# RMS norm weights multiplied before the transposes, evictions by PSUM bank, and tile-by-tile norm between two encoder layers

## Chip, cores and metric

One NeuronCore of a Trainium2 chip (trn2). The metric is device time in microseconds (us) of one execution; lower is better.

## The reference

A two-layer encoder over 256 tokens of width 1024, all in float32. Layer 0 mixes tokens by windowed attention, layer 1 by a gated MLP ("sg", spatial gating); each is followed by a PEER expert mixer. Five RMS norms stand in it, called z = 0 to 4 here: before attention, before the first PEER, before the gated MLP, before the second PEER, and at the end.

```python
def rms_norm(x, g):
    y = xf * lax.rsqrt(jnp.mean(xf * xf, axis=-1, keepdims=True) + NORM_EPS)
    return (y * g).astype(x.dtype)

h = x
for i in range(2):
    hn = rms_norm(h, mix_norm_g[i])
    h = h + (windowed_gqa_attention(hn, ...) if i == 0 else chunked_spatial_gating(hn, ...))
    h = h + peer(rms_norm(h, ffn_norm_g[i]), peer_w_query[i], peer_sub_keys[i], peer_down[i], peer_up[i])
return rms_norm(h, final_norm_g)
```

## The kernel before

The 256 tokens are two tiles (`t` = 0, 1) of 128. Weights stream through the core as "units" of 128 x 1024 numbers, 636 in all. For each unit SyncE (SP) starts a 512 KB transfer into `raw`, ScalarE (ACT) rounds it to `w_hi` (L471), VectorE (DVE) subtracts to get the rest `w_lo` (L725, or L733 in halves), and TensorE (PE) multiplies three times (L1306 to L1308: hi by hi, hi by lo, lo by hi). `w_hi` and `w_lo` have four buffers each. The semaphores `hi_done`, `lo_done` and `used` count units cast, split and multiplied; a unit's buffers come free with `used`. Each engine runs its own instruction list, in the order written, and waits on these counts.

The activations are wanted transposed, also as a hi and a lo part. A norm goes so, with `h` as [tokens, 1024]:

- ACT squares tile 0 and half of tile 1 (L479, L486), DVE the other half (L748), DVE adds epsilon (L744, L751), GpSimd (POOL) takes the power -1/2 (L375, function `root`).
- DVE scales each tile in two halves of 512 columns into `scaled` (L768, `to_scaled`).
- PE transposes 16 blocks of 128 x 128 into PSUM (L1356, `norm_turn`), tile 0 first. At z = 1 and 3 sixteen throw-away transposes (L1346, `fill`) go ahead; at z = 2 they stand between the two tiles.
- For each of eight blocks of 128 columns of `h` (index k), over both tiles, ACT multiplies the PSUM block by the norm's weight (a value per partition, from the small tensor `gains`) and rounds it to `x_hi` (L494), and DVE multiplies again and subtracts into `x_lo` (L779). TURN_ORDER goes through k as 0, 2, 1, 3, ... and ACT waits for DVE's last but one, so that the two read different PSUM banks. PE's first unit takes k in the same order and waits for each `x_lo`.

Around the norms, these queues matter. At the start SP loads `x`, a small table, then weight units. In the attention stage POOL issues the loads of the PEER keys and 28 transfers of 512 KB that clear the `gates` table in DRAM (L388), each paced by `used`; after norm z = 1 four more, and then the store `h_kept` (L432) of 1 MB. DVE overwrites that memory with PEER scores (L1100) and first waits for the store. In the last PEER units of layer 0 (`up` stage), PE takes the last four units for tile 0 first and then for tile 1. The residual (L791) of a tile follows, then norm z = 2, then the "v stage" of the gated MLP: 24 units in six columns of four (`v_columns`), both tiles in each unit.

## Time and profile before

| | |
|---|---|
| runs | 1921.91, 1924.6, 1925.65 us; median 1924.6 |
| profiled execution | 1923.52 us, its span in the trace 1921.7 us |
| busy | PE 98%, DVE 73%, ACT 52%, POOL 36% of the span |
| chain that ended last | PE 80%, ACT 6%, DVE 5%, issue 4%, POOL 4% |
| HBM traffic | 218 GB/s over the span |

The profile is one execution. Its page gives busy time by engine and the costliest groups of instructions, and names for each wait what released it. "L779" is line 779 of the kernel. The granted clock (PEclk) is a share of TensorE's 2.4 GHz: 1.00 or 0.50.

### The profile page before, as it was taken

What the parts mean: (1) busy time and instruction counts of PE and PEld (TensorE: products, weight loads), DVE (VectorE), ACT (ScalarE), POOL (GpSimd) and SP (SyncE); (2) the same over time, 40 slices, a digit from 0 to 9 for tenths busy, and PEclk for the clock granted to TensorE, in tenths of its full rate; (3) what the DMA queues carried; (4) which work ended last, traced back from release to release, by engine and by line L of the source; (5) the groups of instructions that cost most, each with busy time, mean ns of one, the idle gap of its engine ahead of it and who ended that gap; (6) DMA issues with size and microseconds to landing.
All of it is one profiled execution on the core that took longest, in us unless ns stands there. A gap on an engine that the chain in (4) does not pass through costs nothing.

```text
span 1921.7 us, 39006 instructions
## 1 busy us (share of the span) xinstructions
PE 1874.9 (98%) x12114; PEld 1703.6 (89%) x12114; DVE 1397.5 (73%) x3258; ACT 1007.6 (52%) x1638; POOL 696.9 (36%) x627
## 2 busy tenths in 40 slices
PE   7989999999999999999999999999999999999998
PEld 6879999999988888888889989999999988888887
DVE  5858788897467766667567778788897457667666
ACT  4644656656455455454444444666656454454453
POOL 1416687788730000000102106688788740000000
PEclk9999999999999999999999999999999999999999
DMA  6964565565568778996848844566565568778775
GB/s 233 340 249 154 177 185 177 174 179 185 185 217 250 240 240 276 292 304 213 279 159 303 308 155 153 177 185 179 172 186 179 183 206 257 240 239 242 240 241 190
DMA packets 159589, 419.99 MB, mean 219 GB/s; under 512 B 32427, under 2 KB 66251, under 8 KB 159020
## 3 DMA queue, kind: packets, MB, share of 16 engines
q1 hardware_dynamic: 130556, 369.23, 60.7%
q0 software_dynamic: 28976, 50.17, 7.7%
q8 instruction: 16, 0.26, 0.1%
q14 instruction: 41, 0.34, 0.1%
HBM read 382.30 MB, written 37.00 MB: 218 GB/s over the span
## 4 chain that ended last, share of the span: by engine, by line
PE 80%; ACT 6%; DVE 5%; issue 4%; POOL 4%; DMA 1%; SPq 0%; DVEq 0%; POOLq 0%; ACTq 0%
PE psum L1306 26%; PE psum L1308 25%; PE psum L1307 25%; POOL gates L405 4%; ACT L620 2%; ACT w_hi L471 2%; DVE w_lo L733 2%; ACT L662 1%; PE psum L1505 1%; PE psum L1476 1%; ACT big L620 1%; PE psum L1394 0%; DVE big L791 0%; PE psum L1405 0%; PE psum L1431 0%
## 5 line engine op out<-in xcount | busy, mean ns | idle before, releaser
L471 ACT CAST w_hi<-raw 128x1024 fp32r<-128x1024 f32 x636 | 662.9, 1048 | 341.7 <-PE psum L1308 328.8
L1306 PE MATMUL psum<-x_hi,w_hi 128*128 128x256 f32 x2576 | 738.6, 287 | 16.2 <-DVE w_lo L733 13.0
L1307 PE MATMUL psum<-x_lo,w_hi 128*128 128x256 f32 x2576 | 731.2, 284 | 0.0
L1308 PE MATMUL psum<-x_hi,w_lo 128*128 128x256 f32 x2576 | 731.2, 284 | 0.0
L405 POOL DMA_INDIRECT gates<-whole,address x512 | 622.4, 1216 | 246.7 <-issue 148.1
L1306 PEld LDWEIGHTS psum<-x_hi,w_hi 128*128 128x128 f32 x2576 | 496.6, 193 | 27.2 <-issue 12.9
L733 DVE TENSOR_TENSOR w_lo<-raw,w_hi 128x512 fp32r<-128x512 f32 x576 | 369.9, 683 | 178.9 <-ACT w_hi L471 178.5
L1307 PEld LDWEIGHTS psum<-x_lo,w_hi 128*128 128x128 f32 x2576 | 496.8, 193 | 0.9
L1308 PEld LDWEIGHTS psum<-x_hi,w_lo 128*128 128x128 f32 x2576 | 496.4, 193 | 0.0
L1306 PE MATMUL psum<-w_hi,l_hi 128*128 128x512 f32 x1152 | 452.2, 393 | 3.2 <-DVE l_lo L1233 2.2
L1308 PE MATMUL psum<-w_hi,l_lo 128*128 128x512 f32 x1152 | 448.8, 390 | 0.0
L1307 PE MATMUL psum<-w_lo,l_hi 128*128 128x512 f32 x1152 | 448.7, 389 | 0.0
L725 DVE TENSOR_TENSOR w_lo<-raw,w_hi 128x1024 fp32r<-128x1024 f32 x348 | 420.7, 1218 | 18.4 <-ACT w_hi L471 18.4
L652 ACT ACTIVATE big<-psum 128x256 f32<-128x256 f32 x256 | 98.5, 385 | 309.3 <-PE psum L1308 307.0
L1306 PEld LDWEIGHTS psum<-w_hi,l_hi 128*128 128x128 f32 x1152 | 216.7, 188 | 48.7 <-issue 3.9
L1308 PEld LDWEIGHTS psum<-w_hi,l_lo 128*128 128x128 f32 x1152 | 216.5, 188 | 45.4
L1307 PEld LDWEIGHTS psum<-w_lo,l_hi 128*128 128x128 f32 x1152 | 216.7, 188 | 43.8
L1222 DVE TENSOR_TENSOR l_lo<-big,l_hi 128x256 fp32r<-128x256 f32 x248 | 105.5, 425 | 193.5 <-ACT l_hi L670 193.4
L457 POOL DMA_DIRECT2D big<-h_kept x4 | 2.2, 554 | 354.9 <-PE psum L1308 354.9
L1217 DVE TENSOR_TENSOR big<-big,g_t 128x256 f32 (+1 forms) x248 | 103.5, 417 | 5.0 <-DMA g_t<-gates 4.9
L388 POOL DMA_DIRECT2D gates<-zeros x64 | 48.4, 759 | 160.4 <-PE psum L1308 153.7
L670 ACT CAST l_hi<-big 128x256 fp32r (+1 forms) x248 | 98.3, 397 | 0.0
(144 smaller groups left out, 1122.8 us busy)
## 6 DMA issues: line engine op xcount, KB each, us to landing
raw<-in_down SPq DMA_DIRECT2D x256, 512.0 KB
raw<-in_up SPq DMA_DIRECT2D x256, 512.0 KB
raw<-in_sg_units SPq DMA_DIRECT2D x72, 512.0 KB
gates<-zeros POOLq DMA_DIRECT2D x64, 512.0 KB, 7.0
g_t<-gates SPq DMA_DIRECT2D x248, 128.0 KB, 4.5
raw<-in_query SPq DMA_DIRECT2D x32, 512.0 KB
raw<-in_attn_units SPq DMA_DIRECT2D x20, 512.0 KB
gates<-whole,address POOLq DMA_INDIRECT x512
```

The costliest lines, as they stand in the source:

```text
L405: pool.indirect_dma_start(flat, bass.IndirectOffsetOnAxis(address[:, TOPK * m + k:TOPK * m + k + 1], 0), whole[:, t, head, k:k + 1], None, ...
L471: act.copy(w_hi[n % SPLIT][:, :], raw[n % RAW][:, :]).then_inc(hi_done, 1)
L620: act.activation(vals[:, item % 2, :], top1[:, item % 2, :], ACT.Exp, bias=least[:, item % 2:item % 2 + 1], accum_out=sums[:, item % 2:ite ...
L652: act.activation(acts[:, bass.ds(i * group + n, 1), :], p1[n % P1_BANKS].rearrange("p (o t) -> p o t", o=1), ACT.Gelu_apprx_tanh).then_inc ...
L670: act.copy(l_hi[n % GROUP][:, :].rearrange("p (o t) -> p o t", o=1), acts[:, bass.ds(i * GROUP + n, 1), :]).then_inc(l_hi_done, 1)
L725: dve.tensor_tensor(w_lo[n % SPLIT][:, :], raw[n % RAW][:, :], w_hi[n % SPLIT][:, :].bitcast(F32), ALU.subtract).then_inc(lo_done, 1)
L733: ins = dve.tensor_tensor(w_lo[n % SPLIT][:, c], raw[n % RAW][:, c], w_hi[n % SPLIT][:, c].bitcast(F32), ALU.subtract)
L1217: dve.tensor_tensor(a, a, g_t[n % G_TILES][:, :].rearrange("p (o t) -> p o t", o=1), ALU.mult).then_inc(gated_up, 1)
L1222: dve.tensor_tensor(l_lo[n % GROUP][:, :].rearrange("p (o t) -> p o t", o=1), acts[:, bass.ds(i * GROUP + n, 1), :], l_hi[n % GROUP][:, :] ...
L1306: pe.matmul(out_ap, hi_s, hi_m, start=start, stop=False)
L1307: pe.matmul(out_ap, hi_s, lo_m, start=False, stop=False)
L1308: return pe.matmul(out_ap, lo_s, hi_m, start=False, stop=stop)
```

## The change

1. The norm weight is no longer applied after the transposes. A row of 1024 weights, copied to all 128 partitions (`gain_row`, 512 KB), is multiplied in `to_scaled`, by an operation with two tensor inputs. That row is loaded anew for each norm: by SP at the start (z = 0), else by POOL. The small `gains` load is gone.
2. `x_hi` is then a plain copy and `x_lo` a plain subtraction, four of each with 512 columns where there were eight with 256. TURN_ORDER and ACT's wait for DVE are gone; PE waits once per two k.
3. Between the layers, tile 0 is scaled, transposed and split alone. Its transposes stand in PE's list before the last unit's tile 1. The v stage's first column runs tile 0 through units 0 to 3, with tile 1's transposes ahead of unit 3, and then tile 1 through the four units. The sixteen throw-away transposes at z = 2 are gone. The split of v unit 0 is done on POOL, between its two roots, and DVE's next split waits for it.
4. The v stage's first pass is written out on ACT and DVE rather than run as a loop's first turn.

```diff
             for t in range(TT):
                 sp.dma_start(h[:, t, :], x[t * P:(t + 1) * P, :]).then_inc(x_landed, 16)
+            sp.dma_start(gain_row, gains[0].partition_broadcast(P)).then_inc(first_gain_landed, 16)
...
-            pool.dma_start(gains[:, :, :], mix_g).then_inc(const_landed, 16)
...
+            def load_gains(z):
+
+                pool.wait_ge(scaled_done, 4 * z)
+                pool.dma_start(gain_row, gains[z].partition_broadcast(P)).then_inc(gain_landed, 16)
...
             load_keys(0)
+            load_gains(1)
...
-                    roots()
+                    load_gains(3)
...
+                pool.wait_ge(used, up + GAIN_COLUMN + D // T)
+                pool.dma_start(gain_row, (final_g if layer else gains[2]).partition_broadcast(P)).then_inc(gain_landed, 16)
...
+                if layer == 0:
+                    root(slice(0, 1))
+                    n0 = unit0[1]["mix"]
+                    pool.wait_ge(hi_done, n0 + 1)
+                    pool.tensor_tensor(w_lo[n0 % SPLIT][:, :], raw[n0 % RAW][:, :], w_hi[n0 % SPLIT][:, :].bitcast(F32),
+                                       ALU.subtract).then_inc(lo_done, 1)
+                    root(slice(1, 2))
...
-                    dve.tensor_scalar(scaled[:, t, cols], h[:, t, cols], stat[:, 1, t:t + 1], None, ALU.mult
-                                      ).then_inc(scaled_done, 1)
+                    dve.scalar_tensor_tensor(out=scaled[:, t, cols], in0=h[:, t, cols], scalar=stat[:, 1, t:t + 1],
+                                             in1=gain_row[:, cols], op0=ALU.mult, op1=ALU.mult).then_inc(scaled_done, 1)
...
-                    act.wait_ge(turned, 4 * z + k // 2 + 1)
-                    if at > 1:
-                        act.wait_ge(xl_done, KD * z + at - 1)
-                    act.activation(x_hi[:, k, :], turn_at(z, k), ACT.Copy, scale=gains[:, z, k:k + 1]).then_inc(xh_done, 1)
+                    act.wait_ge(turned, TURN_GROUPS * z + at + 1)
+                    source, (k, tok) = turned_part(z, at)
+                    act.copy(x_hi[:, k, tok], source).then_inc(xh_done, 1)
...
-                    dve.scalar_tensor_tensor(out=x_lo[:, k, :], in0=turn_at(z, k), scalar=gains[:, z, k:k + 1],
-                                             in1=x_hi[:, k, :].bitcast(F32), op0=ALU.mult, op1=ALU.subtract
-                                             ).then_inc(xl_done, 1)
+                    dve.tensor_tensor(x_lo[:, k, tok], source, x_hi[:, k, tok].bitcast(F32), ALU.subtract).then_inc(xl_done, 1)
...
+                    def first_column():
+                        for n in range(4):
+                            pe.wait_ge(lo_done, u["mix"] + n + 1)
+                            v_part(n, 0, n % 2 == 0)
+                            if n == 2:
+                                pe.wait_ge(xl_done, TURN_GROUPS * 2 + 2)
+                                turn_tile(2, 1)
+                        for n in range(4):
+                            v_part(n, 1, n % 2 == 0).then_inc(used, 1)
...
                 for c in range(NK - GROUP, NK):
+                    if layer < DEPTH - 1 and c == NK - 1:
+                        turn_tile(2, 0)
                     tile_rows(u["up"] + c, c % GROUP, 1, False, c == NK - 1).then_inc(used, 1)
```

What this does to the order of instructions is seen at three places between the layers. First PE's list, from the last products of the `up` stage (`l_hi`, `l_lo`) to the first of the v stage (`x_hi`), before:

```order
L1307 MATMUL psum<-w_lo,l_hi 128x512
L1308 MATMUL psum<-w_hi,l_lo 128x512
L1356 MATMUL psum<-ident,big 128x128 x8
L1346 MATMUL psum<-ident,x_lo 128x128 x16
L1356 MATMUL psum<-ident,big 128x128 x8
L1306 MATMUL psum<-w_hi,x_hi 128x512
```

And in the changed kernel, where L1350 to L1352 are the three products and L1398 the transposes:

```order
L1352 MATMUL psum<-w_hi,l_lo 128x512
L1398 MATMUL psum<-ident,big 128x128 x8
L1350 MATMUL psum<-w_hi,l_hi 128x512
L1351 MATMUL psum<-w_lo,l_hi 128x512
L1352 MATMUL psum<-w_hi,l_lo 128x512
L1350 MATMUL psum<-w_hi,l_hi 128x512
L1351 MATMUL psum<-w_lo,l_hi 128x512
L1352 MATMUL psum<-w_hi,l_lo 128x512
L1350 MATMUL psum<-w_hi,x_hi 128x512
```

Tile 0's transposes moved ahead of six products of the last unit, the fill is gone, and tile 1's transposes now stand 18 products later, ahead of v unit 3.

Second DVE's list, from the step that starts tile 0's root, before (L748 and L751 are the sum of squares of tile 1):

```order
L744 TENSOR_SCALAR stat<-stat 128x1 [waits sq_done,h_done]
L725 TENSOR_TENSOR w_lo0<-raw0,w_hi0 128x1024 [waits hi_done]
L768 TENSOR_SCALAR big<-big,stat 128x512 [waits rstd_done]
L768 TENSOR_SCALAR big<-big,stat 128x512
L791 TENSOR_TENSOR big<-psum,big 128x512 [waits y_done]
L791 TENSOR_TENSOR big<-psum,big 128x512 [waits used]
L748 ISA big,stat<-big 128x512 [waits h_done]
L748 ISA stat 128x1
L751 SCALAR_TENSOR_TENSOR stat<-stat 128x1 [waits sq_done,d]
L725 TENSOR_TENSOR w_lo1<-raw1,w_hi1 128x1024 [waits hi_done]
L768 TENSOR_SCALAR big<-big,stat 128x512 [waits rstd_done]
```

In the changed kernel, from the same step after tile 0's two scalings (L803 scales, L815 makes `x_lo`, L756 splits, L825 is the residual, L779 and L782 the squares):

```order
L815 TENSOR_TENSOR x_lo<-psum,x_hi 128x4x128 [waits xh_done] x2
L756 TENSOR_TENSOR w_lo1<-raw1,w_hi1 128x1024 [waits hi_done,lo_done]
L825 TENSOR_TENSOR big<-psum,big 128x512 [waits y_done]
L825 TENSOR_TENSOR big<-psum,big 128x512 [waits used]
L779 ISA big,stat<-big 128x512 [waits h_done]
L779 ISA stat 128x1
L782 SCALAR_TENSOR_TENSOR stat<-stat 128x1 [waits sq_done,d]
L756 TENSOR_TENSOR w_lo2<-raw2,w_hi2 128x1024 [waits hi_done]
L803 SCALAR_TENSOR_TENSOR big<-big,stat 128x512 [waits rstd_done]
L803 SCALAR_TENSOR_TENSOR big<-big,stat 128x512
L756 TENSOR_TENSOR w_lo3<-raw3,w_hi3 128x1024 [waits hi_done]
L815 TENSOR_TENSOR x_lo<-psum,x_hi 128x4x128 [waits xh_done] x2
```

The split of v unit 0 left DVE; two halves of `x_lo` and the split of unit 1 now stand ahead of tile 1's residual, and the splits of units 2 and 3 around tile 1's scaling.

Third POOL's list around its two roots, before:

```order
L457 DMA big<-h_kept 128x1024 [waits used] x2
L375 TENSOR_TENSOR stat<-stat,neg_half 128x1 [waits ms_done,rstd_done] x2
L388 DMA gates<-zeros 128x4x256 [waits used] x8
L375 TENSOR_TENSOR stat<-stat,neg_half 128x2 [waits ms_done,rstd_done]
L388 DMA gates<-zeros 128x4x256 [waits used] x24
```

And in the changed kernel (L384 the roots, L479 the split, L396 and L471 loads of weight rows):

```order
L471 DMA big<-in_gains 128x1024 [waits used]
L474 DMA big<-h_kept 128x1024 [waits used] x2
L384 TENSOR_TENSOR stat<-stat,neg_half 128x1 [waits ms_done,rstd_done]
L479 TENSOR_TENSOR w_lo<-raw,w_hi 128x1024 [waits hi_done]
L384 TENSOR_TENSOR stat<-stat,neg_half 128x1 [waits ms_done,rstd_done]
L396 DMA big<-in_gains 128x1024 [waits scaled_done]
L402 DMA gates<-zeros 128x4x256 [waits used] x8
```

A weight row is loaded ahead of `h_kept`, another after the roots, and the split stands between the roots.

## Rows read from the trace of the kernel before

**Rows 1.** The page, part 1: busy time (share of span) and instructions.

```profile
PE 1874.9 (98%) x12114; PEld 1703.6 (89%) x12114; DVE 1397.5 (73%) x3258; ACT 1007.6 (52%) x1638; POOL 696.9 (36%) x627
```

**Rows 2.** Groups by line: busy us, mean ns of one | idle before them, releaser.

```profile
L494 ACT ACTIVATE x_hi<-psum,gains 128x256 fp32r<-128x256 f32 x32 | 13.8, 472 | 12.4 <-PE psum L1356 9.0 <-DVE x_lo L779 3.3 <-issue 0.2
L768 DVE TENSOR_SCALAR big<-big,stat 128x512 f32<-128x512 f32 x16 | 7.2, 502 | 1.2 <-POOL stat L375 1.2
...
L773 DVE SCALAR_TENSOR_TENSOR big<-big,stat 128x512 f32<-128x512 f32 x4 | 2.8, 748 | 1.5 <-POOL stat L375 1.5
L791 DVE TENSOR_TENSOR big<-psum,big 128x512 f32<-128x512 f32 x16 | 10.5, 686 | 3.5 <-PE psum L1308 3.4
L539 ACT COPY big<-psum 128x512 f32<-128x512 f32 x16 | 9.2, 577 | 10.9 <-PE psum L1405 10.8
```

**Rows 3.** Timeline of the start: start us, us, instruction [idle before, releaser].

```profile
10.41 1.05 ACT L471 CAST w_hi<-raw 128x1024 fp32r<-128x1024 f32 x1 [1.74 <-DMA raw<-in_attn_units]
...
12.83 0.88 DVE L779 SCALAR_TENSOR_TENSOR x_lo<-psum,gains,x_hi 128x256 fp32r<-128x256 f32 x2
...
13.46 0.55 PE L1306 MATMUL psum<-x_hi,w_hi 128*128 128x256 f32 x1 [1.10 <-DVE x_lo L779]
...
13.92 0.88 DVE L779 SCALAR_TENSOR_TENSOR x_lo<-psum,gains,x_hi 128x256 fp32r<-128x256 f32 x2 [0.21 <-ACT x_hi L494]
...
17.87 0.38 PE L1308 MATMUL psum<-x_hi,w_lo 128*128 128x256 f32 x1
18.08 0.28 PE L1306 MATMUL psum<-x_hi,w_hi 128*128 128x256 f32 x1
...
32.70 0.69 DVE L818 SCALAR_TENSOR_TENSOR big<-psum,big 128x512 f32<-128x512 f32 x1 [1.79 <-PE psum L1394]
```

**Rows 4.** Windows: stretch, length, POOL busy, PEclk, DMA share, GB/s.

```profile
112.00:116.00 4.00, 0.95 (x2) 1.00 0.99 371
116.00:120.00 4.00, 1.29 (x2) 1.00 0.33 97
```

**Rows 5.** Timeline on POOL, DVE and PE after attention, and one window (PE busy, PEclk).

```profile
118.55 0.75 POOL L388 DMA_DIRECT2D gates<-zeros  x1 [5.60 <-PE psum L1308]
119.29 0.55 POOL L432 DMA_DIRECT2D h_kept<-big  x1
...
127.53 0.42 DVE L1100 COPY big<-psum 128x256 f32<-128x256 f32 x1 [8.81 <-DMA h_kept<-big]
...
129.21 0.58 PE L1306 MATMUL psum<-x_hi,w_hi 128*128 128x256 f32 x1 [4.91 <-DVE w_lo L733]
...
131.00:132.00 1.00, 1.00 (x7) 0.50 0.84 336
```

**Rows 6.** Timeline between the layers: start us, us, instruction [idle before, releaser].

```profile
900.55 0.57 POOL L375 TENSOR_TENSOR stat<-stat,neg_half 128x1 f32<-128x1 f32 x1 [17.82 <-DVE stat L744]
...
903.28 0.39 PE L1308 MATMUL psum<-w_hi,l_lo 128*128 128x512 f32 x1
903.51 1.03 PE L1356 MATMUL psum<-ident,big 128*128 128x128 f32 x8
...
905.24 1.22 DVE L725 TENSOR_TENSOR w_lo<-raw,w_hi 128x1024 fp32r<-128x1024 f32 x1
905.48 1.39 POOL L375 TENSOR_TENSOR stat<-stat,neg_half 128x1 f32<-128x1 f32 x1 [4.35 <-DVE stat L751]
...
907.44 1.09 PE L1356 MATMUL psum<-ident,big 128*128 128x128 f32 x8 [1.15 <-DVE big L768]
...
909.05 0.47 PE L1306 MATMUL psum<-w_hi,x_hi 128*128 128x512 f32 x1 [0.52 <-DVE x_lo L779]
```

**Rows 7.** Timeline of POOL at the start of the program.

```profile
1.50 0.29 POOL L358 TENSOR_SCALAR_AFFINE_SELECT ident<-ident 128x128 f32<-128x128 f32 x1 [0.25 <-POOL big L356]
```

**Rows 8.** Timeline of PE after a wait for ACT, and a window behind it.

```profile
37.75 1.33 PE L1394 MATMUL psum<-big 64*128 64x256 f32 x8 [2.10 <-ACT big L526]
...
39.00:40.00 1.00, 1.00 (x7) 0.50 0.95 373
```

More of the change, by code:

```diff
@@ L39 @@
 ZERO_UNITS = 4
-TURN_ORDER = (0, 2, 1, 3, 4, 6, 5, 7)
+TURN_GROUPS = 4
 FILL = 16
@@ L1316, in transposed @@
                     pe.wait_ge(p1_read, read)
-                for at, k in enumerate(TURN_ORDER):
-                    if norm is not None:
-                        pe.wait_ge(xl_done, KD * norm + at + 1)
+                for k in range(KD):
+                    if norm is not None and k % 2 == 0:
+                        pe.wait_ge(xl_done, TURN_GROUPS * norm + k // 2 + 1)
                     w = slice(k * P, k * P + P)
-                    ins = three(p1[bank], w_hi[s][:, w], w_lo[s][:, w], x_hi[:, k, :], x_lo[:, k, :], at == 0, at == KD - 1)
+                    ins = three(p1[bank], w_hi[s][:, w], w_lo[s][:, w], x_hi[:, k, :], x_lo[:, k, :], k == 0, k == KD - 1)
                 ins.then_inc(used, 1)
@@ L1346, in fill, with turn_tile @@
                     pe.transpose(psum[:, bank, P * (k % 4):P * (k % 4) + P], x_lo[:, k % KD, P:T].bitcast(F32), ident[:, :])
+            def turn_tile(z, t):
+                for k in range(KD):
+                    if k % 4 == 0:
+                        pe.wait_ge(scaled_done, 4 * z + 2 * t + k // 4 + 1)
+                    at = T * (k % 2) + t * P
+                    ins = pe.transpose(psum[:, turn_bank(z, k), at:at + P], scaled[:, t, k * P:(k + 1) * P], ident[:, :])
+                    if k % 4 == 3 if z == 2 else t and k % 2:
+                        ins.then_inc(turned, 1)
             def norm_turn(z):
@@ L1352, in norm_turn @@
                 for t in range(TT):
-                    for k in range(KD):
-                        if k % 4 == 0:
-                            pe.wait_ge(scaled_done, 4 * z + 2 * t + k // 4 + 1)
-                        ins = pe.transpose(turn_at(z, k)[:, t * P:t * P + P], scaled[:, t, k * P:(k + 1) * P], ident[:, :])
-                        if t and k % 2:
-                            ins.then_inc(turned, 1)
-                    if z == 2 and t == 0:
-                        fill(0)
+                    turn_tile(z, t)
             pe.wait_ge(made, 4)
```

98 lines of the change are left out of this document (69 added, 29 removed).

## The prediction

> **What bounds the kernel now.** I read the page's busy times first: PE is busy 1874.9 of 1921.7 us, or 98% [rows 1]. So this change can only win or lose in PE's gaps. All it touches is the five norms and what their new transfers and POOL work collide with. Next I read the groups of the lines that the change rewrites, for prices [rows 2], then the timeline at each place where PE stands still near a norm: the start [rows 3], the stretch after attention, with the DMA windows [rows 4, 5], and the boundary between the layers [rows 6]. The reader should see there that PE waits for three different things: at the start for DVE, which waits for the second weight unit's landing; after attention for the store of `h_kept`; at the boundary for the norm's own chain through DVE, POOL and ACT.
>
> **Prices.** Scaling 128x512 by one tensor costs DVE 502 ns on average, some 0.49 us apart; with two tensors in SBUF the same shape takes a pace of 0.70 us (L773: 2.8 us busy for four) [rows 2]. So each of the four scalings of a norm grows by 0.2 us. `x_hi` was eight times 472 ns and becomes four copies of 577 ns; `x_lo` was eight with the pace 13.92 - 12.83 = 1.09 us per two, since ACT and DVE waited for each other [rows 3], and becomes four of 686 ns, about 0.71 us apart [rows 2]. A product 128x512 takes PE 903.51 - 903.28 = 0.23 us of its time, so six (one v unit, one tile) take 1.36 us [rows 6].
>
> **z = 1 and z = 3 alone.** The transposes that free the first x part come after three scalings: 0.6 us later. The first part takes 0.58 + 0.69 us where it took 0.47 + 0.48: 0.3 us more. So PE's first product starts 0.9 us later. Then `x_lo` takes 3 x 0.71 more instead of 3.27 + 0.55 for the other seven, so the last part is ready 1.7 us sooner after the first; PE then still has two k to do instead of one (0.36 us). Net: 0.9 - 1.7 + 0.36, or -0.5 us each; from both sides, 0 (first product later, PE then bound by itself) and -1.
>
> **The start.** 512 KB of weight rows now go ahead of all weight units on SP's queue. PE's first product (13.46) waits for `x_lo` (12.83), which stands on DVE behind the split of unit 1, and that waits for a transfer until 10.41 [rows 3]. At 371 GB/s and a DMA share of 0.99 [rows 4], 524 KB take 1.4 us. `x_lo`'s first part is 0.2 us longer: PE starts 1.6 us later. It then runs at half rate: two products 128x256 are 18.08 - 17.87 = 0.21 us apart [rows 3], where half of the 0.23 us for 512 columns is 0.12. If the full rate comes at the same time as now, the 1.6 us of lost time are slow time and cost only 0.9. The wider parts don't hurt, since six slow products last longer than the 0.71 between parts. The attention scores (DVE at 32.70) follow PE [rows 3]; the bias table's chain goes through ACT behind the same late unit and may make it 1.4. I take +1.0; the bounds are 0.3 (the transfer fits into a hole) and 3.0 (the full rate comes a step later and 1.6 us more are lost).
>
> **After attention.** POOL's weight row for z = 1 goes into its queue behind the keys and ahead of 28 clearing transfers. The DMA share is 0.99 until 116 and then 0.33 [rows 4]; POOL's last clearing transfer stands still 5.60 us until 118.55, and `h_kept` goes out at 119.29, behind it. DVE waits 8.81 us for it until 127.53 and PE, behind DVE, 4.91 us until 129.21 [rows 5]. This queue has 1.4 us more to move, so the store goes out 1.4 us later; it may land less late than that where it then meets less other traffic. And this is the wait that ends last: what z = 1 wins is lost here, and PE just waits longer. PE restarts at clock 0.50 (131 to 132 [rows 5]), so part of the shift falls again into slow time. I take +0.7; bounds 0.2 and 1.4.
>
> **Between the layers.** Now: PE ends the `up` stage at 903.51, does tile 0's transposes, fill, waits 1.15, transposes tile 1, waits 0.52, and starts the v stage at 909.05 [rows 6]. That is 5.5 us, of which 2.1 are transposes: 3.4 us is the most that could be won. In the new order, tile 0's root ends at 901.1 (900.55 + 0.57 [rows 6]). Scaling ends at 902.6; PE, at the last six products by 902.15, does 8 transposes to 903.2 and the six to 904.6. `x_lo` is ready at 904.2 and 904.9. V unit 0 needs POOL's split. The trace has none. From below it is DVE's own 1.22 us [rows 6]; from above POOL's 0.29 us for 128x128 [rows 7] times eight, 2.3 us; POOL is nearer to its own row, so 2.3. It starts behind DVE's scalings, 902.6, and ends at 904.9. The Trainium skill, "GPSIMD Engine Reference", section 3.1, gives 4497 ns for 2048 columns, which would be an estimate of 2.25 us here.
>
> Then DVE's list is what counts: split of unit 1 to 906.15; residual of tile 1 to 907.5; squares and sum to 908.5; split of unit 2 to 909.65; POOL's root, held as now (905.48 to 906.87 while DVE splits [rows 6]), so scaling from 910.1 to 911.5; split of unit 3 to 912.75; `x_lo` to 914.15. PE does units 0 and 1 until 907.7, waits 2.0 us for the split of unit 2, goes on to 911.05, transposes tile 1 to 912.1, waits for unit 3's split, does it by 914.15 and then tile 1, four times 1.36, until 919.6. Now the first column ends at 909.05 + 48 x 0.227 = 919.95. So of 3.4 us only 0.35 is won: the wait moves from ahead of the v stage into it, because tile 1's norm comes later (910.1 instead of 906.9). Bounds: -2 (PE's pieces fit better) and +1.7 (below).
>
> **Sum.** 1.0 + 0.7 - 0.35 - 0.5 = +0.85 us on the profiled execution's 1923.5, or 1924.4. The median of the runs is 1.1 above that execution, so 1925.5. Tell-apart limit: 0.2% is 3.85 us, 1920.75 to 1928.45.
>
> **Rivals.**
>
> *Slower: POOL's split and DVE's scaling get in each other's way, and PE falls to half rate.* POOL's root ran 1.39 us instead of 0.57 while DVE split two SBUF tensors [rows 6]. The new scaling reads two SBUF tensors as well, and POOL's split starts within 0.2 us of it. If POOL goes ahead of the second half, that half waits up to 2.3 us; all behind it on DVE shifts by 2.0 us, so 1927.5. The Trainium skill, "SBUF — State Buffer", section "Who interferes with whom", says that the second to issue fully blocks; by that rule the 1.39 is right, and either order is possible. PE's idle time of 2.0 us or more at the boundary is that of the 2.10 us at 37.75, behind which the granted clock was 0.50 [rows 8]; a half-rate stretch like the one at the start costs 1.7. Both: 1929.2. With a half-rate stretch it decides from 1.3 us of block on. For it: both patterns are in the rows. Against: DVE starts first by the order of the semaphores.
>
> *Faster: the stall on POOL at 118.55 goes elsewhere.* It stands still for 5.60 us after three transfers, and nothing in the rows names why. With other transfers ahead of it, it may fall on another one. Then `h_kept` goes out up to 5 us sooner and PE's 4.91 us go: 1925.5 - 0.7 - 4.9 = 1919.9. Against: up to that point POOL's queue has as many transfers as before, one removed and one added.
>
> *Faster a little: the boundary works.* Transposes take 2.1 and nothing else waits: 3.4 won instead of 0.35, so 1922.5.
>
> *The weight rows cost nothing* (holes at the start, `h_kept` unmoved): 1923.8.
>
> **Chances.** Forecast as worked out 0.45 (its own range 1924 to 1927.5); block without half rate, or half rate without block, 0.17 (1927.3); both 0.14; rows cost nothing 0.09; boundary works 0.09; POOL's stall goes 0.06. The limits of the terms go across: above 1928.45 lie 0.11 of the case of both, 0.04 of the single ones and 0.03 of the forecast's (a start of 3.0); below 1920.75 lie 0.05 of the last case, 0.03 of the boundary's and 0.01 of the others. That gives slower 0.18, faster 0.09, same 0.73. The range 1920.5 to 1929.5 leaves out some 0.07 above and 0.07 below.
>
> **What the changed profile would show.** Right: PE's first product at about 15 and DVE's wait on a later transfer; the last clearing transfer on POOL near 121 (start's shift included) and PE's restart 1.2 to 2.4 us later; POOL's split 2.3 us long; PE at the boundary with a wait near 2 us ahead of v unit 2; scaling groups at 0.7 us. Wrong: a first product at 13.5; a scaling at the boundary of over 1 us; `h_kept` issued earlier than 119; no wait ahead of unit 2. What would upset the sum most is a clock stretch more or fewer: each is worth 1.7 us, more than any term here.

## The result, and the profile after

The changed kernel takes 1932.38 us (median of 6 runs, 1929.65 to 1934.35) against 1924.74 (6 runs): 7.6 us more, ratio 1.004 with a 95% interval from 1.0026 to 1.0054. So it is slower by more than the 0.2% that can be told from no change. The profiled execution took 1929.65 us with a span of 1927.8. Its page, part 1, answers to [rows 1]: PE is busy 2.6 us less than before, so by this count the whole loss lies in its gaps. (Time at half rate counts as busy; it comes up below.)

```profile
PE 1872.3 (97%) x12098; PEld 1699.6 (88%) x12098; DVE 1398.7 (73%) x3241; ACT 1002.1 (52%) x1622; POOL 698.3 (36%) x630
```

The timeline of the start, against [rows 3]: start us, us, instruction, [idle before, releaser].

```profile
10.99 1.04 ACT L493 CAST w_hi<-raw 128x1024 fp32r<-128x1024 f32 x1 [3.91 <-DMA raw<-in_attn_units]
12.27 1.05 ACT L493 CAST w_hi<-raw 128x1024 fp32r<-128x1024 f32 x1 [0.24 <-DMA raw<-in_attn_units]
13.23 0.57 ACT L523 COPY big<-psum 16x512 f32<-16x512 f32 x1
...
14.10 0.57 POOL L426 DMA_DIRECT2D bias_rows<-big  x1 [5.64 <-ACT big L523]
17.32 1.22 POOL L428 DMA_DIRECT2D big<-bias_rows  x1 [2.65 <-DMA bias_rows<-big]
...
15.79 0.36 PE L1350 MATMUL psum<-x_hi,w_hi 128*128 128x256 f32 x1 [0.75 <-DVE x_lo L815]
15.98 0.28 PE L1351 MATMUL psum<-x_lo,w_hi 128*128 128x256 f32 x1
16.10 0.28 PE L1352 MATMUL psum<-x_hi,w_lo 128*128 128x256 f32 x1
...
35.59 0.69 DVE L852 SCALAR_TENSOR_TENSOR big<-psum,big 128x512 f32<-128x512 f32 x1 [4.38 <-DMA big<-bias_rows]
```

The reader is to see that both weight units land late: unit 0's cast starts at 10.99 (with a wait of 3.91 us) and unit 1's at 12.27, where unit 1 stood at 10.41. PE's first product is 2.33 us late, yet that is nearly all made good (unit 1's products start at 19.45, before at 19.15), because unit 0's products are now 0.12 us apart from the start (15.98, 16.10), where before they were 0.21 apart until 18.08. What is not made good is the last row: VectorE's first scores were released by PE at 32.70 and now wait 4.38 us for the bias table, until 35.59. The table is loaded through a chain that stands behind the units on ScalarE: bias row copy (13.23), store (14.10), load (17.32). Of before, that load:

```profile
15.34 1.22 POOL L414 DMA_DIRECT2D big<-bias_rows  x1 [2.55 <-DMA bias_rows<-big]
```

It landed 16.7 us after its issue, at 32.0, so the table had 0.7 us of slack ahead of the scores. Now it is issued 2.0 us later and takes 18.2 us, and so it lands at 35.5 and is the bound. Behind it PE runs at half rate for longer. Two windows of before and the same two of after; the columns are stretch, length, busy time (count) of PE, PEld, DVE, ACT, POOL, granted clock, DMA share, GB/s:

```profile
39.00:42.00 3.00, 3.00 (x16) 2.99 (x15) 2.86 (x7) 1.83 (x3) 0.00 (x0) 0.51 0.37 143
42.00:46.00 4.00, 3.09 (x30) 2.61 (x30) 3.09 (x11) 2.70 (x12) 0.00 (x0) 1.00 0.27 82
```

```profile
39.00:42.00 3.00, 1.37 (x6) 1.18 (x8) 2.86 (x10) 1.44 (x6) 0.00 (x0) 0.50 0.20 45
42.00:46.00 4.00, 4.00 (x23) 3.36 (x20) 3.15 (x8) 2.21 (x5) 0.00 (x0) 0.61 0.24 97
```

The clock is 0.50 in 39 to 42 in both, but 0.61 against 1.00 in the next four. The stretch after attention, against [rows 5]:

```profile
124.10 0.75 POOL L402 DMA_DIRECT2D gates<-zeros  x1 [7.62 <-PE psum L1352]
124.84 0.55 POOL L447 DMA_DIRECT2D h_kept<-big  x1
...
130.15 0.42 DVE L1139 COPY big<-psum 128x256 f32<-128x256 f32 x1 [9.49 <-DMA h_kept<-big]
...
131.83 0.58 PE L1350 MATMUL psum<-x_hi,w_hi 128*128 128x256 f32 x1 [4.30 <-DVE w_lo L764]
```

PE restarts 2.62 us later than before (131.83 against 129.21), although everything ahead of it comes 3.4 us later: 0.8 us has been absorbed here. The boundary between the layers, against [rows 6] and the L768 row of [rows 2]:

```profile
904.03 3.58 DVE L803 SCALAR_TENSOR_TENSOR big<-big,stat 128x512 f32<-128x512 f32 x2 [0.76 <-POOL stat L384]
...
904.03 2.36 POOL L479 TENSOR_TENSOR w_lo<-raw,w_hi 128x1024 fp32r<-128x1024 f32 x1
...
907.00 1.32 PE L1398 MATMUL psum<-ident,big 128*128 128x128 f32 x8 [1.82 <-DVE big L803]
914.12 0.50 PE L1350 MATMUL psum<-w_hi,x_hi 128*128 128x512 f32 x1 [1.61 <-DVE w_lo L756]
```

Two scalings, 1.4 us elsewhere, take 3.58 us here: the first alone 2.91, the second 0.74. POOL's split of unit 0 runs beside the first of them, from the same hundredth of a microsecond, for 2.36 us.

A ledger of the offset (time after minus time before of the same event) adds it up:

| event | before | after | offset |
|---|---|---|---|
| first scores | 32.70 | 35.59 | +2.89 |
| filler transposes of z = 1 on PE | 107.44 | 110.82 | +3.38 |
| PE restarts behind `h_kept` | 129.21 | 131.83 | +2.62 |
| first residual between the layers | 897.65 | 900.52 | +2.87 |
| first gelu of the v stage | 920.31 | 924.24 | +3.93 |
| filler transposes of z = 3 on PE | 1125.53 | 1130.88 | +5.35 |
| first query copy behind z = 3 | 1135.94 | 1141.31 | +5.37 |
| first residual of the last norm | 1909.45 | 1915.56 | +6.11 |

The step from +3.93 to +5.35 goes with a longer stretch at half rate, behind a gap of 2.9 us that both kernels have after the v stage. The last step, from +5.37 to +6.11, falls at the start of layer 1's `up` stage: ScalarE waits 2.39 us for its second unit (cast at 1582.83), where before it waited 1.15 (1576.71), and PE then stands still for 0.92 us, where before it had no wait. Windows behind the v stage, of after and of before:

```profile
987.00:990.00 3.00, 1.43 (x5) 1.36 (x6) 2.79 (x7) 1.50 (x3) 0.00 (x0) 0.54 0.48 175
990.00:993.00 3.00, 3.00 (x8) 2.31 (x7) 2.93 (x8) 2.25 (x3) 0.00 (x0) 0.50 0.53 180
993.00:996.00 3.00, 3.00 (x19) 2.71 (x18) 1.68 (x2) 0.05 (x1) 0.00 (x0) 0.83 0.44 131
```

```profile
984.00:987.00 3.00, 2.45 (x8) 2.16 (x9) 2.75 (x7) 0.75 (x3) 0.00 (x0) 0.51 0.32 116
987.00:990.00 3.00, 3.00 (x17) 2.58 (x16) 2.97 (x6) 2.04 (x3) 0.00 (x0) 0.92 0.46 169
990.00:993.00 3.00, 3.00 (x26) 2.91 (x25) 0.95 (x2) 0.38 (x1) 0.00 (x0) 1.00 0.75 225
```

### The profile page after: what moved, and what is told of

It is laid out like the page before. It is cut to its first block, busy times and chain, and to the rows that moved or that the text cites. A ratio compares the mean times of both kernels' runs of the same rounds, so it can differ in the third digit from the quotient of the medians.

```text
span 1927.8 us, 38875 instructions
## 1 busy us (share of the span) xinstructions
PE 1872.3 (97%) x12098; PEld 1699.6 (88%) x12098; DVE 1398.7 (73%) x3241; ACT 1002.1 (52%) x1622; POOL 698.3 (36%) x630
## 4 chain that ended last, share of the span: by engine, by line
PE 79%; ACT 6%; DVE 4%; issue 4%; POOL 4%; DMA 2%; SPq 0%; DVEq 0%; POOLq 0%; ACTq 0%
PE psum L1350 26%; PE psum L1352 25%; PE psum L1351 25%; POOL gates L419 3%; ACT L645 2%; ACT w_hi L493 2%; DVE w_lo L764 2%; ACT L687 1%; DMA big<-bias_rows 1%; PE psum L1575 1%; ACT big L645 1%; PE psum L1546 1%; DMA raw<-in_attn_units 0%; PE psum L1452 0%; DVE big L825 0%
## 5 line engine op out<-in xcount | busy, mean ns | idle before, releaser
L1350 PE MATMUL psum<-x_hi,w_hi 128*128 128x256 f32 x2576 | 736.6, 286 | 15.1 <-DVE w_lo L764 12.5
L1352 PE MATMUL psum<-x_hi,w_lo 128*128 128x256 f32 x2576 | 729.9, 283 | 0.0
L1350 PEld LDWEIGHTS psum<-x_hi,w_hi 128*128 128x128 f32 x2576 | 495.2, 192 | 24.4 <-issue 14.8
L1352 PEld LDWEIGHTS psum<-x_hi,w_lo 128*128 128x128 f32 x2576 | 495.4, 192 | 0.0
L1350 PE MATMUL psum<-w_hi,l_hi 128*128 128x512 f32 x1152 | 452.8, 393 | 4.1 <-DVE l_lo L1272 2.2
L1352 PE MATMUL psum<-w_hi,l_lo 128*128 128x512 f32 x1152 | 449.4, 390 | 0.0
L756 DVE TENSOR_TENSOR w_lo<-raw,w_hi 128x1024 fp32r<-128x1024 f32 x347 | 420.2, 1219 | 22.0 <-ACT w_hi L493 21.8
L1350 PEld LDWEIGHTS psum<-w_hi,l_hi 128*128 128x128 f32 x1152 | 216.9, 188 | 49.3 <-issue 3.9
L1352 PEld LDWEIGHTS psum<-w_hi,l_lo 128*128 128x128 f32 x1152 | 216.7, 188 | 45.9
L471 POOL DMA_DIRECT2D big<-in_final_g x1 | 0.6, 579 | 295.4 <-PE psum L1352 295.4
```

Of the source, the lines that this page charges most:

```text
L756: dve.tensor_tensor(w_lo[n % SPLIT][:, :], raw[n % RAW][:, :], w_hi[n % SPLIT][:, :].bitcast(F32), ALU.subtract).then_inc(lo_done, 1)
L1350: pe.matmul(out_ap, hi_s, hi_m, start=start, stop=False)
L1352: return pe.matmul(out_ap, lo_s, hi_m, start=False, stop=stop)
```

## The experiments

The variants ran on other chips than the first measurement. There every kernel, the one before too, takes some 80 us more (2005 to 2009 us), in gaps of the PEER stages that the first chip does not have, and the runs scatter more. Totals are therefore given as ratios to the kernel before on the same chip. The changed kernel itself was run beside its variants on one of these chips only (`after_again`), so the ratios of the other variants can't be set against its own. Single terms are read in the traces, where the length of the boundary repeats well and the start roughly. One such gap, in `after_again` and then in the first trace of the same kernel (columns as above):

```profile
171.00:181.00 10.00, 6.09 (x29) 5.80 (x30) 7.91 (x30) 2.63 (x4) 3.87 (x4) 0.54 0.27 79
```

```profile
171.00:181.00 10.00, 9.65 (x79) 9.25 (x78) 7.79 (x31) 5.78 (x11) 7.95 (x7) 1.00 0.43 134
```

PE is busy 6.09 of these 10 us on the one chip, at clock 0.54, and 9.65 on the other. Why the chips differ was not looked into.

**Is the weight row the start's loss?** `no_row_at_start` leaves the 512 KB row of norm 0 out (set to 1.0: norm 0's weights are left out of the result).

```diff
-            sp.dma_start(gain_row, gains[0].partition_broadcast(P)).then_inc(first_gain_landed, 16)
+            dve.memset(gain_row, 1.0).then_inc(first_gain_landed, 1)
```

> The changed kernel without the weight row's transfer at the start: DVE fills the row with ones, so norm z = 0 goes without its weights (that part is left out). Theory A, the 512 KB at the head of SP's queue push the small table and the first weight units back, the bias table goes out 2.0 us later (17.32 instead of 15.34) and DVE waits 4.38 us for it: DVE's first attention score is back near 32.7 (35.6 with the row), its wait for the bias table is gone or under 0.5 us, and the whole is 2.5 to 3.5 us faster than the changed kernel, about 4 to 5 us slower than before. Theory B, the start's loss comes from the wider scaling and the parts by bank: the score stays near 35, and the time moves less than 1 us.

`before_plus_row` is the other way round: the kernel before, with an unused row of the same size loaded behind `x`.

```diff
+            sp.dma_start(gain_row, final_g.partition_broadcast(P)).then_inc(early_landed, 16)
```

> The kernel before with one thing added: SP loads a 512 KB row of weights right behind x, which nothing at the start reads. Theory A (the transfer's place in the queue costs, not its use): 2.5 to 3.5 us slower than before, DVE's first attention score near 35.5 with a wait for the bias table. Theory B (only the norm that waits for it costs): within 1 us of before.

Ratios to before: 1.0034 (1.0010 to 1.0058) and 1.0012 (0.9991 to 1.0034). Both expectations missed at the scores (34.56, not 32.7; 33.97, not 35.5). ScalarE's cast of unit 0 and VectorE's first scores, without the row:

```profile
11.07 1.04 ACT L492 CAST w_hi<-raw 128x1024 fp32r<-128x1024 f32 x1 [3.73 <-DMA raw<-in_attn_units]
...
34.56 0.69 DVE L852 SCALAR_TENSOR_TENSOR big<-psum,big 128x512 f32<-128x512 f32 x1 [2.06 <-DMA big<-bias_rows]
```

And with the row added to the kernel before:

```profile
10.64 1.04 ACT L473 CAST w_hi<-raw 128x1024 fp32r<-128x1024 f32 x1 [3.42 <-DMA raw<-in_attn_units]
...
33.97 0.69 DVE L820 SCALAR_TENSOR_TENSOR big<-psum,big 128x512 f32<-128x512 f32 x1 [2.31 <-DMA big<-bias_rows]
```

Without the row unit 0 is as late as with it, 11.07, though the kernel before had it at 7.63. With the row alone added to before it comes at 10.64. So the row is enough to make unit 0 late, and yet not needed: something else in the changed kernel does it as well.

**The sink.** The change also drops a 16 KB load at the head of POOL's queue. The next one there, the sink (16 numbers copied to all 128 partitions, 8 KB in rows of 64 bytes), is so issued at 2.21 instead of 2.94. `sink_late` moves it behind the bias rows' store, and the step that reads it on VectorE down; `sink_late_no_row` also leaves norm 0's weights out as above.

```diff
-            pool.dma_start(sink_in, sink.partition_broadcast(P)).then_inc(const_landed, 16)
...
             pool.dma_start(bias_rows, bias_row_sb[0:HEADS, :]).then_inc(bias_stored, 16)
+            pool.dma_start(sink_in, sink.partition_broadcast(P)).then_inc(const_landed, 16)
             pool.wait_ge(bias_stored, 16)
```

> The changed kernel, with the load of the sink (one 64-byte row to all 128 partitions) moved on POOL's queue from the top of the program to behind the store of the bias rows, and VectorE's one step on it moved behind the first seven splits. Everything else, the 512 KB weight row at the start too, stays. Theory S: units 0 and 1 of the weights land late (their ScalarE casts at 10.99 and 12.27 us, against 7.63 and 10.41 before) because the sink's packets now go ahead of unit 0, with the small load gone that stood ahead of it. Then unit 0's cast starts by about 9 us, unit 1's by about 11.5, the bias row copy by about 12.5 instead of 13.23, and VectorE's first scores at about 34.5 instead of 35.59; total about 1 to 3 us under the changed kernel. Rival R: it is the 512 KB row itself that takes the transfer engines before unit 0 and the bias table; then the casts stay within 0.5 us of 10.99 and 12.27, the scores at 35.2 to 35.8, and the total does not move.

> The same with the weight row's load at the start left out as well: the row is set to 1.0, so that norm 0's weights are left out of the result. If row and sink together are the start's whole loss, unit 0's cast starts at about 7.6 us, unit 1's at 9 to 10.4, the bias row copy at 11 to 11.4, PE's first product at 14 to 14.5 and VectorE's first scores at 32.4 to 33.0, which is the kernel before's 32.70. If something else delays them (the vector scaling, the new split order), the casts still come at 7.6 and the scores at 33.5 or later. With the row alone left out the scores came at 34.56.

Ratios: 1.0010 (0.9979 to 1.0042) and 1.0017 (0.9989 to 1.0045), too wide to tell anything. The timelines tell it. With the sink late (theory S came out in part: the casts are 1.4 us earlier, but unit 0 is not back by 9 us and the scores not by 34.5):

```profile
9.57 1.05 ACT L493 CAST w_hi<-raw 128x1024 fp32r<-128x1024 f32 x1 [2.53 <-DMA raw<-in_attn_units]
...
17.02 1.19 POOL L428 DMA_DIRECT2D big<-bias_rows  x1 [3.02 <-DMA bias_rows<-big]
...
34.99 0.69 DVE L852 SCALAR_TENSOR_TENSOR big<-psum,big 128x512 f32<-128x512 f32 x1 [4.76 <-DMA big<-bias_rows]
```

With both out of the way, units, copy and scores all come as early as expected or earlier:

```profile
7.28 1.05 ACT L492 CAST w_hi<-raw 128x1024 fp32r<-128x1024 f32 x1 [0.29 <-DMA raw<-in_attn_units]
8.56 1.05 ACT L492 CAST w_hi<-raw 128x1024 fp32r<-128x1024 f32 x1 [0.24 <-DMA raw<-in_attn_units]
...
12.71 1.19 POOL L427 DMA_DIRECT2D big<-bias_rows  x1 [0.99 <-DMA bias_rows<-big]
...
31.89 0.69 DVE L852 SCALAR_TENSOR_TENSOR big<-psum,big 128x512 f32<-128x512 f32 x1 [2.79 <-DMA big<-bias_rows]
```

The same rows of all traces, those of the runs told below too (ScalarE's cast of unit 0, VectorE's first scores):

| ahead of unit 0 | cast of unit 0 | first scores |
|---|---|---|
| neither: kernel before, sink issued at 2.94, unit 0 at 2.58 | 7.63 | 32.70 |
| both: kernel before with the row added, sink at 2.94, unit 0 at 3.06 (`before_plus_row`) | 10.64 | 33.97 |
| neither, sink moved away (`sink_late_no_row`; `before_best`, `after_best`) | 7.28; 7.64, 7.62 | 31.89; 31.24, 33.76 |
| row only (`sink_late`) | 9.57 | 34.99 |
| sink only (`no_row_at_start`; `row_by_pe`) | 11.07; 10.55 | 34.56; 36.38 |
| both (five traces with the changed kernel's start) | 10.84 to 11.47 | 35.08 to 37.22 |

Against the 7.6 of neither, the row alone makes unit 0 2.0 us late, the sink alone 2.9 to 3.5, both together 3.0 to 3.9: the two overlap, so taking one away gives back less than it costs alone: 1.4 us at unit 0 for the sink, nothing for the row. `before_plus_row` also shows that in the changed kernel the row by itself is enough to let the sink go ahead: with the `gains` load still in place, unit 0's load is issued at 3.06 instead of 2.58, behind the sink's at 2.94, and unit 0 is 3.0 us late. The dropped load matters once the row is gone, as in `no_row_at_start`. The five traces of the same start scatter by 2.1 us at the scores, so that what one alone does there (34.56, 34.99, just under their lowest) is not settled. That both together are about the start's whole loss is shown by 31.89, with only these two altered, against 32.70 in before and 31.24 in `before_best`, which has neither ahead. At most 0.7 us, less than the scatter, is left for the new way of norming. Why the scores of the changed kernel come 1.1 us or more behind those of `before_plus_row`, with unit 0 at most 0.8 us later, stays open. In the kernel before, the sink's load is issued behind unit 0's and it is unit 1 that is late: with the sink moved away (`before_best`) its cast is at 8.91, not 10.41.

The same traces show the clock. Time at 0.50 between 30 and 50 us comes as none, 3.4 or 6.8 us. Where VectorE waited 4.4 us or more ahead of its first scores (six traces) it was 6.8. Where it waited 3.1 or less (eight) it was 3.4 or none, but for one, `sink_late_no_row`, with 6.8 after 2.79.

**Put the bias chain first.** `bias_first` has SP load the two small tables ahead of the row, and ScalarE copy the bias row ahead of its casts.

```diff
-            sp.dma_start(gain_row, gains[0].partition_broadcast(P)).then_inc(first_gain_landed, 16)
             sp.dma_start(table[0:BUCKETS, :], rel_table).then_inc(table_landed, 16)
             sp.dma_start(bucket_sb[0:BUCKETS + 1, :], bucket_map).then_inc(table_landed, 16)
+            sp.dma_start(gain_row, gains[0].partition_broadcast(P)).then_inc(first_gain_landed, 16)
...
+            act.wait_ge(bias_row_pe, 1)
+            act.copy(bias_row_sb[0:HEADS, :], psum[0:HEADS, 4, :]).then_inc(bias_row_done, 1)
             for n in range(AHEAD):
                 split_hi(n)
```

> The changed kernel with the bias table's chain ahead of the rest at the start: SP's two small loads for it stand ahead of the 512 KB row, and ScalarE copies the bias row before it casts units 0 and 1. Theory B: the first scores wait only for the bias table, which is late by what its chain was late. Then PE's bias product ends at about 8 us, the copy starts at 8 to 9 instead of 13.23, the table's load at about 13, and the first scores go at 31.9 to 32.6 with hardly a wait on the table (they then follow PE's products, at about 31.8); the slow clock after that wait is shorter, and the total is 4 to 7 us under the changed kernel, at or just under the kernel before. Rival: the table's transit of 17 us is set by the transfers it shares the engines with, so that an earlier issue brings no earlier landing; then the scores stay after 34.5 and the total moves by less than 2 us.

The expectation missed. Ratio 1.0013 (0.9986 to 1.0039), first scores at 37.70, released by PE. ScalarE's copy, VectorE's scaling and POOL's table load:

```profile
9.89 0.57 ACT L521 COPY big<-psum 16x512 f32<-16x512 f32 x1 [2.79 <-PE psum L1411]
...
11.57 2.74 DVE L803 SCALAR_TENSOR_TENSOR big<-big,stat 128x512 f32<-128x512 f32 x4 [3.95 <-DMA big<-in_gains]
...
16.07 1.22 POOL L428 DMA_DIRECT2D big<-bias_rows  x1 [4.74 <-DMA bias_rows<-big]
```

The copy came 3.3 us earlier, but the store behind it was slow (POOL waits 4.74 us for it) and the row itself now ended the wait of the scaling: 3.95 us, until 11.57 instead of 7.95. Unit 0's cast came at 12.82, later than in any other run, and the scores then waited for PE. So the order of the issues moved the loss from one waiter to the next; the bytes and the sink are still there.

`row_by_pe` takes the bytes away and keeps the computation: 4 KB to one partition, spread by two products of a row of ones.

```diff
-            sp.dma_start(gain_row, gains[0].partition_broadcast(P)).then_inc(first_gain_landed, 16)
+            sp.dma_start(gain_row[0:1, :], gains[0:1, :]).then_inc(first_gain_landed, 16)
...
+            for half in range(2):
+                ins = pe.matmul(psum[:, 2 + half, :], ones[0:1, :], gain_row[0:1, 512 * half:512 * half + 512], start=True, stop=True)
+            ins.then_inc(row_spread, 1)
```

> The changed kernel with only one thing altered: the weight row of norm 0 comes as 4 KB to one partition, and TensorE, idle then, spreads it over the partitions with two products of a row of ones, into two banks that VectorE's scaling reads. The computation is whole. Theory R (the 512 KB of the row are 1 us of the loss, the sink ahead of unit 0 the rest): the first scores go at 34.3 to 34.9, like with the row left out (34.56), the scaling no later than 8.5. Rival: the two products and the scaling out of PSUM cost what the transfer did, and the scores stay at 35.5 or later. The total is 0 to 2 us under the changed kernel's.

The ratio is 1.0007 (0.9981 to 1.0033), the scores 36.38, as the rival had it: nothing gained. PE's spreading and the scaling behind it:

```profile
5.46 3.75 PE L1416 MATMUL psum<-big 1*128 1x512 f32 x4 [5.46 <-DMA big<-in_gains]
...
9.25 2.72 DVE L806 SCALAR_TENSOR_TENSOR big<-big,stat,psum 128x512 f32<-128x512 f32 x4 [1.58 <-PE psum L1416]
```

Two products of half a row take four passes and 3.75 us, so the scaling starts 1.3 us late. Unit 0 comes at 10.55 all the same, since the sink is still ahead of it. Where it is not (`after_best`, below), the price of spreading shows: the bias row copy comes at 11.21, behind PE, against 9.51 with the row left out.

**The boundary.** `split_on_dve` takes POOL's split back to VectorE, behind tile 0's scaling. `old_boundary` restores the whole order of before between the layers (its throw-away transposes and the v stage's loop too) under the new way of norming.

```diff
-                    pool.tensor_tensor(w_lo[n0 % SPLIT][:, :], raw[n0 % RAW][:, :], w_hi[n0 % SPLIT][:, :].bitcast(F32),
-                                       ALU.subtract).then_inc(lo_done, 1)
...
                     to_scaled(0)
+                    split_lo(u["up"] + NK)
                     norm_parts(z, (0, 1))
```

> The changed kernel with the split of v unit 0 back on DVE, behind tile 0's scaling; POOL does only its roots between the layers. Theory A, POOL's split holds DVE's scaling (two of them took 3.58 us, and POOL's split 2.36): the two scalings take 1.41 us, the second residual starts about 1 us earlier on DVE in spite of the 1.2 us that the split takes there, and the whole is 1 to 2 us faster than the changed kernel. Theory B, the scaling is slow for a reason of its own (its place in memory, or PE and ACT traffic): it stays at 3.58 us and the whole gets 1.2 us slower.

> The changed kernel with the order of before between the layers: both tiles normed together, throw-away transposes between them, split of unit 0 on DVE, v stage with both tiles in each unit; weights by rows and evictions by bank stay. Theory A (the tile-by-tile order costs): the v stage's first column ends about 1 to 1.5 us earlier than in the changed kernel, so 1 to 1.5 us faster. Theory B (it saves, and the loss is all elsewhere): slower than the changed kernel.

VectorE with the split taken back, at the place of the 3.58 us row above:

```profile
951.56 1.42 DVE L799 SCALAR_TENSOR_TENSOR big<-big,stat 128x512 f32<-128x512 f32 x2 [0.77 <-POOL stat L384]
952.89 1.22 DVE L752 TENSOR_TENSOR w_lo<-raw,w_hi 128x1024 fp32r<-128x1024 f32 x1
```

PE has no wait ahead of tile 0's transposes then, where the changed kernel has one of 1.82 us. The length from tile 0's first residual to the first gelu of the v stage, which repeats within 0.1 us:

| kernel | us |
|---|---|
| before (and with store and sink moved, below) | 22.66, 22.7 |
| after, seven traces with its boundary | 23.71 to 23.74 |
| after, split on VectorE (`split_on_dve`, `after_best`) | 21.84, 21.86 |
| after, order of before (`old_boundary`) | 23.73 |

Two more traces are longer, with a clock that fell inside this stretch: `before_plus_row` with 24.3 (0.76 for five of its us) and `bias_first` with 24.1 (0.86 for twelve). The clock alone does not explain them: it fell inside the stretch in `no_row_at_start` and `sink_late_no_row` too, and these have 23.73 and 23.74. POOL's split beside the scaling costs 1.9 us: without it the scaling takes 1.42 us again. The new order is worth 1.9, the new way of norming costs 1.1, and the three together make the +1.1 of the ledger. Neither theory of `old_boundary` had this: the length is that of the changed kernel, since what the new order gains and what POOL's split costs are the same size. The totals, 1.0032 (1.0010 to 1.0054) for `split_on_dve` and 1.0050 (1.0026 to 1.0075) for `old_boundary`, point the same way but overlap.

**The store behind the queue.** `store_first` issues `h_kept` ahead of the last four clears.

```diff
-                if layer == 0:
-                    clear(0, range(28, NK // ZERO_UNITS), lambda q: ATTN_UNITS)
                 pool.wait_ge(h_done, 4 * (2 * layer + 1))
                 pool.dma_start(h_kept, h.rearrange("p t d -> p (t d)")).then_inc(h_stored, 16)
+                if layer == 0:
+                    clear(0, range(28, NK // ZERO_UNITS), lambda q: ATTN_UNITS)
```

> The changed kernel with POOL's store of h issued ahead of the last four clears of the gates instead of behind them (layer 0). It tests the step on h_kept: VectorE's score copy waits 9.49 us for this store, which POOL issues at 124.84, behind a clear that waits 7.62 us for room in the queue. Theory Q: the wait goes with the queue; the store is issued at about 114, waits behind the packets of the clears already in the queue and lands at 119 to 124, PE's wait of 4.30 us goes to 0 to 1.5, the slow clock after it goes too, and the total is 3 to 7 us under the changed kernel. Rival: the queue's packets go in order and the store, issued earlier, lands no earlier than now (at about 130); the total is unchanged within 1.5 us.

Ratio 0.9994 (0.9970 to 1.0019), and 2006.4 us against 2009.9 to 2010.6 of the three variants that ran beside it. POOL and VectorE:

```profile
115.39 0.59 POOL L445 DMA_DIRECT2D h_kept<-big  x1
...
125.45 0.42 DVE L1139 COPY big<-psum 128x256 f32<-128x256 f32 x1 [3.60 <-PE psum L1575]
```

VectorE's copy is released by PE and not by the store, 5.9 us closer to the first query copy than in the changed kernel; PE has no wait there and the clock stays at 1.00. From the first query copy to the fourth (the "keys copy" of the expectations below) it takes 9.51 us instead of 16.42 (before 16.85). The expected 3 to 7 us are there at this place. POOL's stall is not gone, it falls on clears that nobody waits for: after the store and two clears it stands still for 6.27 us (at 123.75), as it did after three clears.

**Everything together.** `after_best` is the changed kernel with store first, sink late, split on VectorE and the row spread by PE; `before_best` is the kernel before with store first and sink late, none of the change in it. `after_again` is the changed kernel beside them.

> The changed kernel itself, unaltered, beside its variants on one chip. It should stand at 1.002 to 1.005 of the kernel before, as in its first measurement, with the first scores at 35 to 37 us behind the bias table and a wait of 4 to 5 us on TensorE at about 132.

> The changed kernel with all that the runs so far point to: the row of norm 0 spread by TensorE, the sink loaded behind the bias rows' store, POOL's store of h ahead of the last four clears, and unit 0's split between the layers on VectorE. If the effects add, the first scores go at 31.7 to 32.3 (with row and sink out of the way: 31.89), the fourth keys copy on ScalarE comes about 9.5 us after the first instead of 16.4, the stretch between the layers (first residual to first gelu of the v stage) takes 21.9 instead of 23.7, and the total is 11 to 14 us under the changed kernel and 4 to 9 us under the kernel before. Rival: they overlap, since a start that is 3.5 us earlier meets the same transfers later; then it stands within 2 us of the run with the store alone moved, at 0.999 to 1.0 of the kernel before.

> The kernel before with the two moves that are not part of the change: the sink loaded behind the bias rows' store and the store of h ahead of the last four clears. If the store's wait is as it is in the changed kernel, the fourth keys copy comes about 9.5 us after the first instead of 16.85, the slow clock at 127 to 134 us goes, and the first scores come at 31.5 to 32.7; total 6 to 9 us under the kernel before, at 0.995 to 0.997 of it. It then tells whether the changed kernel's way of norming is worth anything once both have these moves: with it better by 1 to 2 us the v stage's stretch pays, with it level or worse nothing of the change is left.

| kernel | median, us | ratio to before, 95% interval |
|---|---|---|
| before | 2009.14 | |
| after_again | 2013.07 | 1.0012 (0.9981 to 1.0043) |
| after_best | 1999.0 | 0.9947 (0.9922 to 0.9973) |
| before_best | 1997.72 | 0.9947 (0.9918 to 0.9975) |

The first scores, of after_best and then of before_best:

```profile
33.76 0.69 DVE L852 SCALAR_TENSOR_TENSOR big<-psum,big 128x512 f32<-128x512 f32 x1 [3.04 <-DMA big<-bias_rows]
```

```profile
31.24 0.69 DVE L821 SCALAR_TENSOR_TENSOR big<-psum,big 128x512 f32<-128x512 f32 x1 [2.21 <-DMA big<-bias_rows]
```

Both gain some 10 us on the kernel before, a bit more than expected, and the changed way of norming adds nothing to that: its boundary is 0.8 us shorter (21.9 against 22.7), and its scores come 2.5 us later, behind the row's spreading. Of what was expected, the first scores of `after_best` missed (33.76, not 31.7 to 32.3) and those of `before_best` came just under their range (31.24 for 31.5 to 32.7); the fourth query copy (9.50 and 9.51 us after the first) and the boundary came in. Which of the moves gives how much of the 10 us is shown at the places named, not in the totals. `after_again` stands lower than in the first measurement, 1.0012 for 1.004, with an interval that holds both, and no change too.

## Why the prediction was wrong

The forecast was 1925.5, no change, range 1920.5 to 1929.5; it is 1932.4. By its own steps:

- **The start, +1.0 (bounds 0.3 to 3.0): +3.4 at the end of the attention stage, the step that failed most.** I let the attention scores follow PE and allowed the bias table's chain 0.4 us on top of that. The scores follow the table: +2.89, and 0.5 more by the end of the stage, behind a longer stretch at half rate. The slack could have been read in the trace of before: the table landed at 32.0, 0.7 us ahead of the scores. PE's own path came near the number by another way: it is 2.33 us late (forecast 1.6) and 0.30 of it is left at unit 1 (forecast 0.9), because the slow products in which I let it make up time did not come at all. Two sizes were wrong. I priced the row's bytes at 1.4 us; alone they make unit 0 2.0 us late. And I gave no price to the sink, which alone is worth about 3 us: the row pushes unit 0's issue behind it, and the `gains` load that I took off without a term moves it up as well. The runs show that row and sink are about the whole of it.
- **z = 1 and 3, -0.5 each:** -0.13 from the filler transposes to the first query copy at z = 1 (10.25 to 10.12 us), nothing at z = 3 (+5.35 to +5.37). PE's first product comes 1.2 and 1.1 us later (forecast 0.9), and that takes back nearly all that the wider parts of `x_lo` win.
- **After attention, +0.7 (0.2 to 1.4): -0.76.** The issue did slip, by 2.2 us beyond the late start (118.55 to 124.10, with a stall of 7.62 for 5.60; it is 7.5 to 8.6 in the other traces with the changed queue, 5.88 in `before_plus_row`), but the store then landed in 5.3 us instead of 8.2, which I had allowed for only as far as the issue's slip. Since this wait ends at a transfer, it swallowed part of the late start. That it is the wait that ends last here, as I said, `store_first` shows.
- **Between the layers, -0.35 (-2 to +1.7): +1.06.** PE waits 1.61 us ahead of v unit 2, forecast 2.0, and POOL's split took 2.36 us, forecast 2.3. The term failed on one point, which was the rival: POOL's split and VectorE's scaling get in each other's way, and PE waits 1.82 us ahead of tile 0's transposes, where I had no wait. I priced the block at 2.0 us; it costs 1.9. Without it the boundary is 0.8 us shorter than before, next to my 0.35. I had POOL's split begin behind the scalings, at 902.6, but nothing in its list holds it there: it starts right behind the root, in the same hundredth of a microsecond as the scaling, and the scaling waited. The Trainium skill, "SBUF — State Buffer", section "Who interferes with whom", says that the second to issue is blocked entirely. The trace agrees in so far as one of the two waits for nearly all of the other: the first scaling takes 2.91 us instead of 0.74, beside a split of 2.36. Which of them was issued first it can't show.
- **Clock stretches: the text named them as the largest upset, and they came, but not where I put them.** The boundary has none (1.00 throughout in after). Behind the scores and behind the v stage the stretch at 0.50 grew from 3.4 to 6.8 us. I priced one at 1.7 us; in the ledger they show as +0.5 and +1.4. Behind the scores the longer wait goes with it, with one exception. Behind the v stage PE's gap is the same, and why the stretch is longer there is not settled.
- **Not in the forecast:** +0.7 us at the start of layer 1's `up` stage, where a unit of weights lands later; why it does stays open. The 1.5 us between the profiled execution's difference (6.1) and that of the medians (7.6) were not traced.

The rival "POOL's stall goes" is refuted by 7.62 us at 124.10, "the rows cost nothing" by the table of the start; "the boundary works" is half true, once the split is off POOL.

## What to carry to other kernels

When a change adds or removes a transfer at the start, list every chain that crosses the same queues and engines, with its slack, and price the one with the least; the chain that waits now is not always the one that waits next. Adding or removing a transfer changes which of two queues issues first: a small load may now go ahead of something larger that it used to follow. Look for a wait on a transfer that was issued late because of queue order before reworking arithmetic: moving two issues on POOL gave 0.5% (`before_best`), and with them in place the whole reordering of the norm gave nothing more.

## What was unexpected of the hardware

- A load of 8 KB in 64-byte rows to 128 partitions took 6.8 us from issue to landing in before and 7.4 in after, against 3.9 for each 512 KB of `x`, and what is issued behind it is late: with it alone ahead, unit 0's cast comes about 3 us later, more than the 2.0 us of the 512 KB row.
- POOL's TENSOR_TENSOR over 128x1024 in SBUF, beside VectorE's operation with two SBUF tensors, took 2.36 us, and the two scalings 3.58 instead of 1.42: VectorE lost 2.16 us, nearly as long as the split.
- Time at 0.50 behind a gap of TensorE came as 3.4 or 6.8 us at the two places looked at, not in proportion to the gap: behind the v stage the same gap of 2.9 us was followed by 3.4 us in before and 6.8 in after. The longer stretch cost 0.5 us more at one place and 1.4 at the other.
- A float32 product of one row by 512 columns took as long as one of 33 rows: 3.75 us for two, against 1.86 us for one.
